# Normalising joins: when a quarter is added to x, and by which token tile the last products run

## What is computed

```
def rms_norm_2(x, g):
    xf = x.astype(jnp.float32)
    y = xf * lax.rsqrt(jnp.mean(xf * xf, axis=-1, keepdims=True) + RMS_EPS)
    return (y * g.astype(jnp.float32)).astype(x.dtype)
...
    for i in range(DEPTH):
        g = norm_g[i]
        h = h + 0.5 * rms_norm_2(swiglu(rms_norm_2(h, g[0]), ffn_w13[i, 0], ffn_w2[i, 0]), g[1])
        hn = rms_norm_2(h, g[2])
...
        h = h + rms_norm_2(m, g[3])
        h = h + 0.5 * rms_norm_2(swiglu(rms_norm_2(h, g[4]), ffn_w13[i, 1], ffn_w2[i, 1]), g[5])
        gate = jax.nn.sigmoid(rms_norm_2(h, g[6]) @ ple_w_gate[i])
        h = h + rms_norm_2(gate * (p[i] @ ple_w_proj[i]), g[7])
```

## Time and profile before

| | |
|---|---|
| median of three runs | 2205.34 us |
| profiled execution, its own time | 2206.7 us |
| its span, first to last instruction | 2204.8 us |
| TensorE busy | 2125.8 us, 96% |
| VectorE busy | 1520.7 us, 69% |
| ScalarE busy | 1153.5 us, 52% |
| GpSimd busy | 352.7 us, 16% |
| mean granted TensorE clock | 0.988 |

### The profile page before, as it was taken

The page is one execution under the profiler, slowest core; times in us unless marked ns, Lnnn a source line. Parts: engine busy times, 40 slices in busy tenths (PEclk is TensorE's granted clock), DMA queues, the critical chain, the costliest instruction groups (busy, mean ns, idle before and its releaser), DMA issues.

```text
span 2204.8 us, 38908 instructions
## 1 busy us (share of the span) xinstructions
PE 2125.8 (96%) x13508; PEld 1807.4 (82%) x13508; DVE 1520.7 (69%) x2388; ACT 1153.5 (52%) x1986; POOL 352.7 (16%) x449
## 2 busy tenths in 40 slices
PE   8999899999999899999999999999999899889998
PEld 7888778887888678888887988888788678768886
DVE  6666956667667956666667757666766777677666
ACT  5445745445456644455455446446645554445445
POOL 1111111112111111112111001111211102301111
PEclk9999999999999999999999999999999999999999
DMA  6555426555555336555556555556555441115553
GB/s 246 199 184 182 139 91 206 186 196 171 187 184 191 131 99 202 184 181 189 183 190 220 191 172 162 192 185 235 182 186 185 164 133 63 61 68 191 193 184 123
DMA packets 104110, 375.53 MB, mean 170 GB/s; under 512 B 11696, under 2 KB 12208, under 8 KB 104016
## 3 DMA queue, kind: packets, MB, share of 16 engines
q1 hardware_dynamic: 104016, 374.24, 50.9%
HBM read 373.15 MB, written 1.05 MB: 170 GB/s over the span
## 4 chain that ended last, share of the span: by engine, by line
PE 82%; DVE 10%; ACT 4%; issue 2%; POOL 1%; DMA 1%; SPq 0%; DVEq 0%; ACTq 0%; POOLq 0%
PE bank L843 27%; PE bank L847 14%; PE bank L186 12%; PE bank L187 11%; PE bank L188 11%; DVE w_lo L180 3%; DVE work L1358 1%; ACT w_hi L173 1%; ACT act L462 1%; PE bank L376 1%; PE bank L2060 1%; DMA work<-pt_dram 1%; ACT work L424 0%; DVE act L567 0%; PE bank L2043 0%
## 5 line engine op out<-in xcount | busy, mean ns | idle before, releaser
L843 PE MATMUL bank<-act,w_hi 128*128 128x512 f32 x2816 | 709.3, 394 | 3.7 <-ACT w_hi L173 2.2
L843 PEld LDWEIGHTS bank<-act,w_hi 128*128 128x128 f32 x2816 | 519.6, 190 | 107.4 <-DVE act L567 3.0
L757 DVE TENSOR_TENSOR w_lo<-raw,w_hi 128x1024 fp32r<-128x1024 f32 x432 | 502.8, 1219 | 3.3
L748 ACT ACTIVATE w_hi<-raw 128x1024 fp32r<-128x1024 f32 x432 | 425.0, 1050 | 2.4
L847 PEld LDWEIGHTS bank<-act,w_lo 128*128 128x128 f32 x2816 | 385.0, 191 | 27.8
L847 PE MATMUL bank<-act,w_lo 128*128 128x256 f32 x2816 | 393.1, 282 | 0.0
L180 DVE TENSOR_TENSOR w_lo<-raw,w_hi 128x1024 fp32r<-128x1024 f32 x248 | 295.1, 1220 | 70.6 <-ACT w_hi L173 70.4
L813 DVE TENSOR_TENSOR work<-bank,work 128x256 f32<-128x256 f32 x176 | 74.7, 424 | 386.4 <-ACT work L775 386.4
L790 POOL TENSOR_TENSOR work<-work,rb 128x256 f32<-128x256 f32 x176 | 129.6, 736 | 1048.2 <-DVE work L810 1046.2
L186 PE MATMUL bank<-w_hi,g_hi 128*128 128x512 f32 x704 | 277.1, 394 | 0.8
L187 PE MATMUL bank<-w_lo,g_hi 128*128 128x512 f32 x704 | 276.0, 392 | 0.0
(11 more groups left out here) (278 smaller groups left out, 2222.1 us busy)
## 6 DMA issues: line engine op xcount, KB each, us to landing
raw<-w_dram SPq DMA_DIRECT2D x680, 512.0 KB, 4.4
work<-rows_dram SPq DMA_DIRECT2D x13, 512.0 KB, 6.5
work<-rrows_dram SPq DMA_DIRECT2D x5, 512.0 KB, 3.3
x<-x_dram SPq DMA_DIRECT2D x2, 512.0 KB, 4.0
out<-x SPq DMA_DIRECT2D x4, 256.0 KB, 2.1
work<-g_dram SPq DMA_DIRECT2D x1, 640.0 KB, 9.9
work<-dist_dram SPq DMA_DIRECT2D x2, 256.0 KB, 5.3
work<-ws_dram SPq DMA_DIRECT2D x1, 512.0 KB, 8.5
```

The source lines that it names most:

```text
L748: nc.scalar.activation(c.w_hi[:, n % RING, :], c.raw[:, n % RING, :], ACT.Copy).then_inc(c.hi_ready, 1)
L757: nc.vector.tensor_tensor(c.w_lo[:, n % RING, :], c.raw[:, n % RING, :], c.w_hi[:, n % RING, :].bitcast(F32), ALU.subtract).then_inc(c.lo_ ...
L843: nc.tensor.matmul(bank[:, :], c.w_hi[:, slot(m), k * P:(k + 1) * P], c.act[:, k, :, :], start=k == 0, stop=False)
```

## The change

Three things are changed.

**1. Joins behind an FFN** (1, 3, 5, 7): VectorE adds a quarter as soon as the root of its token tile is there, between the gains (`by_rows_vector`). In join 1 the fourth add stands behind two low parts, and the fourth quarter's transposes stand in the next stage, behind its first unit's 12 products (`last_turn_inside`).

**2. Joins behind output products and the embedding** (2, 4, 6, and 8): `token_first`. The last four units of the output products, and the gate's half 1, run for token tile 0 first and then for token tile 1. The adds go in `ROWS` order. Token 0's mean, root and two adds stand ahead of token 1's last quarter (`first_token_vector`, `first_token_scalar`). In 2 and 6 TensorE transposes both of token 0's quarters ahead of the last unit's products for token tile 1, in 4 one of them. The fourth quarter's transposes stand inside the FFN, behind its first two tiles. Tiles 4 to 7 use other banks. In 8 nothing is transposed.

**3.** `PLACE` becomes `place`, and the calls from the old code for `early` joins are gone from `project_stage` (no join of that kind comes there).

In `Join`:

```diff
+        self.adds = self.ROWS if token_first else self.QUADS
+        self.place = [5, 7, 5, 7, 0, 1, 0, 1] if token_first else [5, 7, 5, 7, 0, 2, 0, 2]
...
     def tensor(self, pe):
-        while self.turned < 4:
+        while self.turned < (3 if self.last_turn_inside() else 4):
             self.turn(pe)
...
+    def last_turn_inside(self):
+
+        return self.row is not None and self.plain is None and not self.units_first
...
         if k % 4 == 0:
-            act.wait_ge(s["turned"].sem, s["turned"].at(2 + k // 2))
+            act.wait_ge(s["turned"].sem, s["turned"].at(self.adds.index((1, k // 4)) + 1))
...
+        if self.token_first:
+            self.square(act)
+            for k in range(4):
+                self.high(act)
         self.first_half_scalar(act)
...
+    def first_token_scalar(self, act):
+
+        while self.y_squared < 3:
+            self.square_y(act)
+        while self.squared < 2:
+            self.square(act)
+
+    def first_token_vector(self, dve):
+
+        while self.y_gained < 2:
+            dve.wait_ge(self.s["y_squares"].sem, self.s["y_squares"].at(self.y_gained + 1))
+            self.gain_y(dve)
+        self.mean_y(dve, 2)
+        if self.y_gained < 3:
+            self.gain_y(dve)
+        self.add_y(dve)
+        self.add_y(dve)
+
+    def second_token_vector(self, dve):
+        if self.y_gained < 4:
+            self.mean_y(dve, 3)
+            self.gain_y(dve)
+        self.add_y(dve)
+        self.add_y(dve)
+
+    def by_rows_vector(self, dve):
...
+        gain()
+        self.mean_y(dve, 1)
+        gain()
+        self.add_y(dve)
+        self.mean_y(dve, 3)
+        gain()
+        self.add_y(dve)
+        gain()
+        self.add_y(dve)
+        if self.last_turn_inside():
+            self.low(dve)
+            self.low(dve)
+        self.add_y(dve)
```

In `ffn_stage`, TensorE, in the loop over the tiles:

```diff
             for k in half:
+                if k == 2 and join.turned < 4:
+                    join.turn(pe)
                 join.tile_there(pe, k)
```

In `project_stage`, TensorE:

```diff
-            for k in range(per):
+            for k in range(per if h == 0 else per - 4):
                 product_a(c, pe, first + h * per + k, k, per, [c.bank[h], c.bank[2 + h]], tile0,
                           there if h == 0 else None, quad)
-                if h == 1 and k == 0 and out.early:
+        for t in range(NT):
+            for k in range(per - 4, per):
+                if (t, k) == (1, per - 1):
                     out.turn(pe)
                     out.turn(pe)
+                unit_there(c, pe, first + per + k)
+                last = product_t(c, first + per + k, k, per, [c.bank[1], c.bank[3]], t, tile0)
+                if t == 1:
+                    last.then_inc(c.unit_used, 1)
+            if t == 0:
+                last.then_inc(quad.sem, 1)
```

In `ple_stages`, TensorE, then ScalarE, then VectorE:

```diff
+        for t in range(NT):
             for k in range(4):
...
+                if (t, k) == (1, 3) and turns:
+                    out.turn(pe)
...
+                if h == 1:
+                    out.square_y(act)
+                if h == 1 and t == 0 and turns:
+                    out.square(act)
+                    out.square(act)
...
-                if h == 1 and t == 1:
-                    out.mean_y(dve, 2)
                 out.gain_y(dve)
+                if h == 1 and t == 0:
+                    out.first_token_vector(dve)
```

In `gmlp_stage`, TensorE:

```diff
+                if n == 0 and k == 0:
+                    join.turn(pe)
```

71 lines of the change are left out of this document (34 added, 37 removed).

## The result

The changed kernel takes 2220.58 us (median of 5 runs, 2219.82 to 2222.21), the kernel before 2208.05 in the same comparison (5 runs, 2203.42 to 2210.34). The ratio is 1.0057, with a 95% interval of 1.0045 to 1.0069: slower by 0.57%, or 12.5 us. The forecast was slower, 2215.5 with a range of 2208 to 2220, so the direction is right and the time lies 0.6 above the range. Later comparisons gave the kernel before medians from 2207.03 to 2209.13 (9 to 23 runs), so the 2205.34 to which the forecast added its sum was itself 2 to 4 us low. The sum of differences was +10.25 where 12.5 was measured; the changed kernel, run again, gave 1.0062 (1.0048 to 1.0075), 13.8 us.

What follows compares the result with a forecast made beforehand. TensorE, busy 96% of the span, was taken as the bound, so any wait is paid in full. Terms -0.9 + 0.5 + 4.5 + 3.7 + 1.7 + 0.75 = +10.25 us on 2205.34 gave 2215.5, range 2208 to 2220.

Steps and rivals of the forecast that it cites:

- Finish, -0.9: Join 8: token 0's two adds are done while token 1's products run, so the last output transfer comes 0.9 us earlier.
- Joins 3, 5 and 7, +0.25 each: VectorE's adds stand between the gains, so the fourth add ends 0.25 us later in each, delaying what follows.
- Join 1, +1.7: Later fourth-quarter transposes delay ScalarE's high parts and weight splits; TensorE waits 1.6 us for w_lo, costing 1.7 us.
- Joins 2, 4 and 6, +0.5, +3.7, +4.5: Join 2: later low parts, fourth-quarter transposes among products; joins 4, 6: gain-row chains delay transposes 2.3 and 2.8 us; half clock included.
- the clock term: Extra half-clock stretches: none in join 2, one more in join 4, two or three instead of one in join 6, +1 to +2.
- The fourth turn: Fourth quarter's four transposes stand among the first gate products; tail order costs 0.5 us in joins 2, 4 and 6.
- (a): Gain row lands in time in joins 4 and 6, which cost 0.5 to 1 each: +3 to +4, 2209; chance 0.11.
- (b): Shorter idle stretches leave the clock full in the joins, waits stay: +3, 2208.5; chance 0.04.
- (c): Two adds and their transposes leave the tail, nothing else binds: -4 to -5, 2201; chance 0.06.
- (d): Late splits of join 1's kind also occur behind joins 4 and 6: over +14, 2220; chance 0.06.
- what would show it: Waits in joins 4, 6 and 1; transposes' waits not below 12.7 us; finish adds 0.9 closer; more half-clock stretches.
- the two signs of being wrong: No wait ahead of the last unit in joins 4 and 6, or first gate products closer behind the last output product.

Runs made afterwards that it cites:

- e5: Changed kernel with the fourth quarter's transposes ahead of the first products again in joins 1, 2, 4, 5 and 6; ratio to before 1.0034.
- e6: Changed kernel with ScalarE's splits of the next two weight units ahead of high parts 4 to 7 in joins 1, 2, 4, 6; ratio 1.0056.
- e1: Changed kernel with gain rows of joins 2, 4, 6 and the finish issued ahead of their stage's last four weight units; ratio to before 1.0041.
- e11: Changed kernel with matmuls of no use filling TensorE's idle times in joins 2, 4 and 6; ratio to before 1.0037.
- e8: Kernel before with the changed finish, and matmuls of no use filling idle time before the first transposes in joins 1, 2, 4, 5, 6; ratio 0.9988.
- e4: Kernel before with only the finish and the last embedding's gate products by token changed; ratio to before 0.9993.
- e10: Kernel of e9 with matmuls of no use filling TensorE's idle time in joins 1, 2, 4 and 6; ratio to before 1.0006.
- e9: Changed kernel with gain rows issued early and the fourth quarter's transposes ahead of the products again; ratio to before 1.0016.

## Why the prediction was right in direction, and where it failed

*Finish, -0.9.* Right: -0.95 in two kernels.

*Joins 3, 5 and 7, +0.25 each.* Join 5 measures +0.2. The other two can't be told from the noise between executions.

*Join 1, +1.7.* The mechanism is right, the wait was 1.6 forecast and 1.43 measured, and e5 takes it all away. The size is +2.2 to +3.4 against the old joins: the four largest of the six steps (e6 among them) have a second half-clock stretch in them, worth 1.1 us.

*Joins 2, 4 and 6, +0.5, +3.7, +4.5.* The waits were forecast at 2.3 in join 4 (2.91 and 2.33 measured) and 2.8 in join 6 (1.75 and 1.92; the row came 0.9 sooner after its issue, 6.5 us for the 7.4 of the earlier trace rows, and in nine profiles with this row at its old place it took 6.4 to 6.9: the one execution that was read had the slowest). The order of the chain, from the gain row over VectorE's and ScalarE's queues to the adds, is as forecast, and e1 shows it. The terms "at an unchanged clock" were good: with the clock full in both orders (e11 against e8) the new one is slower by 0.5, 3.1 and 2.5 us; the prediction had 0.5, 2.8 and 3.0 to 3.5.

*The step that failed is the clock term.* In join 2 it was "with one half-clock stretch in either", so nothing, in join 4 "one more half-clock stretch", 0.9, in join 6 "+1 to +2". Measured by profiles, the clock costs 1.6, 4.0 and 2.4 us in the new order (e11), and 0.9, 0.8 and 0.5 to 0.7 in the old (e8): 5.6 to 5.8 more, where the sum had some 2 to 2.4. By the runs' times it is 4.4 to 5.5 against 1.1 (e8 against e4), so 3.3 to 4.4 more, which is also above the forecast, though their intervals are wide. Join 4 has most of it: 3.2 us more for the 0.9 forecast. In join 6 two errors met: the wait forecast 0.9 to 1.05 us too long, and the clock too cheap. That the measured 3.8 to 5.1 there (against the old joins) has the forecast 4.5 in it is luck. The number of stretches was only slightly off (1, 3 and 1 in the first profile, 1, 4 and 2 in the second; forecast 1, 2, and 2 or 3). What was wrong is above all their price in the new order against the old. A reading of the timelines, which no run tests by itself: in the old order a half-clock stretch lies over first products that wait for low parts anyway, which absorbs some of it; in join 4's new order it lies over six output products that had nothing to wait for, and in all three over transposes on which high parts, low parts, splits and products hang.

On this the Trainium skill, in "TensorE: Matmul & The Clock Gate", Terms, was nearer in the total: the throttled time times the missing half, 1.7 us for a stretch, gave +13 in the prediction, and 12.5 and 13.8 were measured. By the stretch this case's runs don't agree with it: one cost 0.5 to 0.9 us in the kernel before (e8), 1.1 in join 1 of the changed one, and on average 1.3 in its joins 2, 4 and 6 (8.0 us in five and seven stretches). So the agreement of the total is in part luck. The prediction explained the gap between 1.7 and its own 1.3 by waits of TensorE in the stretch; its row has TensorE busy for 3.40 of 3.40 us, and the 1.3 had left out the transposes in it.

*The fourth turn.* The prediction let the four transposes of the fourth quarter stand among the products for 0.5 us in join 2, and carried the 0.5 over to joins 4 and 6. e5 gives back 1.1, 2.4 to 3.0 and 0.6 to 1.9 for them, half clock included. At full clock in both, join 2 with them (e11) is only 0.4 behind join 2 without (e10), which agrees with the 0.5; the rest is the clock again.

*The rivals.* (a), the gain row doesn't bind, is refuted by e1, and (b), the clock stays full, by the windows. The argument against (b), that no idle stretch gets shorter than 2.3, was false for joins 1 and 5, where 2.31 became 1.03, 0.87 and 0.60; the clock halved there all the same. (c), faster because adds leave the tail, by e9 and e10: the tail's idle time was never made of them. (d), more than forecast, is nearest in size, but not by its mechanism: what came on top were half-clock stretches, not late splits behind joins 4 and 6.

*The signs.* All of "what would show it" came true in kind. But so did one of the two signs of being wrong: the first gate products start 4.22 us behind the end of the last output product in joins 2 and 6, for 5.10 and 5.60 before. The prediction's own working for join 2 had 4.2 for 5.1. The sign was ill chosen: it looks at the first product alone, while the old order had all transposes done by then.

*The base.* The sum was added to a median of three runs. Of the 5.1 us between forecast and measured time, 2.7 are the kernel before, which measured 2208.05 beside the changed one; the rest is the sum itself.

What stays open is how much of join 4's and join 6's clock cost belongs to the wait ahead of the transposes and how much to the tail; e11 filled both at once.

## What to carry to other kernels

Taking work out of a tail helps only if the tail is made of that work. Here a chain of mean, root and one add set the wait of TensorE, and the other adds had run beside what followed. Before moving a consumer forward, look at everything that its producer's queue holds ahead of it, transfers too: a gain row that landed harmlessly late stood on the path as soon as its adds were wanted ahead of the last six products. And an idle stretch in the middle of a dense run of products can cost more than its length: in join 4 the waits and the clock behind them cost about 3 and 4 us. Where such a wait can't be avoided, matmuls without use that end just before it does are worth a try; here they gave 0.5 to 0.9 us in each of four old joins and cost nothing that the times show.
